# Attention steps of one head and 128 queries in a hybrid trunk layer, with gates, conv taps and weight sums moved

## The chip, the cores and the metric

The kernel runs on one core of one Trainium2 chip. The metric is the device time of one launch in microseconds (us), taken several times; the profile is one execution, read engine by engine: TensorE (PE, with its weight loads as PEld), VectorE (DVE), ScalarE (ACT), GpSimd (POOL) and SyncE (SP), which here only issues transfers. Each engine runs its own list of instructions in order, and the lists meet at semaphores.

## The reference, cut to what matters

```
u = layer_norm(x) * (1 + sc_m) + sh_m                       # x: 1024 tokens x 1024
z_pool, z_q, z_k, z_v, z_conv, z_gate = split(u @ w_in)     # 256, 3 x 512, 512, 3 x 1024 columns
y_pool = pool_mixer(z_pool) @ w_br_pool                     # causal means over 2, 4, 8, 16 tokens
y_attn = chunk_attention(z_q, z_k, z_v, rel_bias) @ w_br_attn   # 8 heads of 64, own chunk of 64 + 8 before
y_conv = conv_module(z_conv) @ w_br_conv                    # GLU, causal depthwise conv of 31 taps, LN, swish
gates = sigmoid(z_gate + b_gate)
merged = gates[0] * y_pool + gates[1] * y_attn + gates[2] * y_conv
x = layer_norm(ALPHA * x + g_m * (merged @ w_o))
u = layer_norm(x) * (1 + sc_f) + sh_f
x = layer_norm(ALPHA * x + g_f * (square(relu(u @ w_ff1 + b_ff1)) @ w_ff2 + b_ff2))
```

In the attention, softmax runs over the 576 keys of a chunk's band (fewer at the start), with a bias that depends on the clipped distance.

## The kernel before

All matmuls that carry precision take fp32 data cut in two fp32r parts, high and low, made by ACT (a copy that rounds) and DVE (what is left). A product of two such tensors is three matmuls: high x high, high x low, low x high (`product`, L1971). Weights come in blocks of 128 columns: SP loads one to `w_raw`, ACT cuts `w_hi`, DVE cuts `w_lo`, PE uses it in 8 x 2 x 3 = 48 matmuls of 512 columns. Raw, high and low each have two buffers, so block n + 2 is cut when PE has finished block n.

The order of the work on PE: blocks 0 to 5 (conv and pool inputs), blocks 6 to 8 (q, k, v of the first pair of heads), and then the attention, 4 pairs of 16 steps. A step `a` is one chunk of 64 queries of both heads of the pair. The 128 stationary rows hold both heads' features, with zeros where a query of one head meets the other (`q_block`; POOL writes the zeros). `scores` (L2126) are three products over up to 576 keys, in two parts of 288 where they are all there. DVE adds the bias and takes the maximum (L1523), ACT takes Exp and the sum (L997), DVE inverts and scales (L1537, L1538), PE transposes (L2158), ACT and DVE cut the transposed probabilities (`pt_hi`, `pt_lo`, L1544), and every second step `weigh` (L2161) multiplies them with v, 3 matmuls of 256 columns for each block of 128 keys; ACT copies two 64-row pieces out. Between these, `between` (L2209) puts matmuls that project the next pair, 9 in a step, half after the scores and half after the transposes; in the last pair they are those of two gate blocks (`EARLY = 2`), 6 in a step. Within a step, PE's order is scores(a), fillers, weigh, transposes of a - 1, fillers.

DVE also runs the 62 conv taps (L1428, 128 x 1024 each): 9 before the attention and nearly all others in its steps, but not in those after which a block is cut.

After the attention PE does a third early gate block, the pool matmuls and the conv sums, then for each of 8 output columns of 128 (j) three gate blocks and one block of branch weights. Gates 0 to 2 go through ACT's sigmoid (`gate`), DVE multiplies the branch results in PSUM with them and adds. The last column is written out by hand, with branches ahead of gates.

POOL makes the pooling means before the attention, and from the first branch results on it makes the weight sums of the second MLP matrix for a Winograd form: 16 steps (L772 to L791) each load 1 MB of `w_ff2`, scale it by the gate row (two products of 128 x 1024, L778), make four sums of 128 x 512 and store 1.75 MB to `tw_scratch`. The MLP then reads them.

Semaphores named below: `biased`, `probs_done`, `pt_lo_done` (steps of the attention), `w_lo_done` (blocks cut), `h_free` (a projection's bank read), `sig_done`, `y_used`, `tw_stored`.

## Time and profile before

| | us |
|---|---|
| median of 3 runs | 1448.37 (1446.94 to 1448.57) |
| span of the profiled execution | 1445.0 |
| time of the runs beside that span (median) | 3.4 more |
| TensorE clock granted, mean over the span | 0.999 of full |
| first scores of the attention, scores of its last step | 156.8, 386.2 |
| POOL's first and last product of the weight sums | 453.6, 659.6 |

The span goes from the first to the last instruction of the profile; a run's time holds also what lies around it. The profile names instructions by line of the kernel and by the tensors that they write and read. A PE row's duration includes the time in which the matmul drains and overlaps with the next, so the price of a matmul is the distance between the starts of two rows. For the other engines a duration is nearly the time that the instruction holds its engine, waits on a shared port included.

### The profile page before, as it was taken

What the parts mean: (1) busy time and instruction counts of PE and PEld (TensorE: products, weight loads), DVE (VectorE), ACT (ScalarE), POOL (GpSimd) and SP (SyncE); (2) the same over time, 40 slices, a digit from 0 to 9 for tenths busy, and PEclk for the clock granted to TensorE, in tenths of its full rate; (3) what the DMA queues carried; (4) which work ended last, traced back from release to release, by engine and by line L of the source; (5) the groups of instructions that cost most, each with busy time, mean ns of one, the idle gap of its engine ahead of it and who ended that gap; (6) DMA issues with size and microseconds to landing.
All of it is one profiled execution on the core that took longest, in us unless ns stands there. A gap on an engine that the chain in (4) does not pass through costs nothing.

```text
span 1445.0 us, 17546 instructions
## 1 busy us (share of the span) xinstructions
PE 1426.1 (99%) x6770; PEld 1175.9 (81%) x6770; DVE 966.1 (67%) x1242; ACT 586.8 (41%) x829; POOL 455.4 (32%) x381
## 2 busy tenths in 40 slices
PE   7999999999999999999999999999999999999997
PEld 1788888888878888888888898888888888888886
DVE  4888888887785355453468888666555744575594
ACT  3412455555562112112435765444444544443251
POOL 1003500000004889895014415533443302040011
PEclk9999999999999999999999999999999999999999
DMA  9873111101014676776451283544445868576361
GB/s 349 295 265 114 31 30 38 38 16 32 16 44 162 245 259 249 255 268 218 131 204 59 88 277 131 175 154 160 156 137 192 277 243 306 210 233 231 113 224 58
DMA packets 149267, 241.49 MB, mean 167 GB/s; under 512 B 9480, under 2 KB 79550, under 8 KB 147144
## 3 DMA queue, kind: packets, MB, share of 16 engines
q1 hardware_dynamic: 134968, 177.04, 36.7%
q0 software_dynamic: 14224, 63.45, 11.6%
q8 instruction: 47, 0.77, 0.2%
q14 instruction: 28, 0.23, 0.1%
HBM read 170.17 MB, written 70.29 MB: 166 GB/s over the span
## 4 chain that ended last, share of the span: by engine, by line
PE 96%; DVE 1%; DMA 1%; SPq 1%; ACT 0%; issue 0%; DVEq 0%
PE ps L1974 27%; PE ps L1976 27%; PE ps L1975 27%; PE ps L2102 10%; PE ps L2158 2%; DMA mid<-in_x_dram 1%; PE ps L2041 1%; PE ps L2328 0%; SPq L455 0%; DVE bn L1331 0%; PE ps L1993 0%; PE ps L2123 0%; PE ps L2017 0%; PE ps L2200 0%; PE ps L2194 0%; PE ps L2022 0%
## 5 line engine op out<-in xcount | busy, mean ns | idle before, releaser
L1974 PE MATMUL ps<-act_hi,w_hi 128*128 128x512 f32 (+1 forms) x512 | 198.0, 387 | 0.0
L1976 PE MATMUL ps<-act_hi,w_lo 128*128 128x512 f32 (+1 forms) x512 | 196.0, 383 | 0.0
L1975 PE MATMUL ps<-act_lo,w_hi 128*128 128x512 f32 (+1 forms) x512 | 195.9, 383 | 0.0
L1839 DVE TENSOR_TENSOR part_lo<-k_raw,part_hi 128x1024 fp32r<-128x1024 f32 x112 | 153.9, 1414 | 48.2 <-ACT part_hi L872 46.5
L1974 PE MATMUL ps<-part_hi 128*128 128x512 f32 x448 | 174.3, 389 | 0.0
L1975 PE MATMUL ps<-part_lo,part_hi 128*128 128x512 f32 x448 | 174.3, 389 | 0.0
L1976 PE MATMUL ps<-part_hi,part_lo 128*128 128x512 f32 x448 | 174.3, 389 | 0.0
L872 ACT ACTIVATE part_hi<-k_raw 128x1024 fp32r<-128x1024 f32 x112 | 116.3, 1059 | 108.6 <-DMA k_raw<-tw_scratch 84.5
L1571 DVE TENSOR_TENSOR w_lo<-w_raw,w_hi 128x1024 fp32r<-128x1024 f32 x30 | 73.1, 2436 | 123.9 <-ACT w_hi L872 123.8
L1974 PEld LDWEIGHTS ps<-act_hi,w_hi 128*128 128x128 f32 x512 | 96.2, 188 | 19.7 <-issue 1.4
L1975 PEld LDWEIGHTS ps<-act_lo,w_hi 128*128 128x128 f32 x512 | 96.3, 188 | 19.1 <-issue 0.7
L1976 PEld LDWEIGHTS ps<-act_hi,w_lo 128*128 128x128 f32 x512 | 96.2, 188 | 18.9
L1975 PEld LDWEIGHTS ps<-part_lo,part_hi 128*128 128x128 f32 x448 | 84.1, 188 | 17.6
L1974 PEld LDWEIGHTS ps<-part_hi 128*128 128x128 f32 x448 | 84.1, 188 | 17.4
L1976 PEld LDWEIGHTS ps<-part_hi,part_lo 128*128 128x128 f32 x448 | 84.1, 188 | 17.4
L2102 PE MATMUL ps<-act_lo,w_hi 128*128 128x512 f32 x224 | 92.0, 411 | 0.0
L1251 ACT ACTIVATE h_buf<-h_buf,cols 128x1024 f32<-128x1024 f32 x28 | 32.3, 1152 | 144.7 <-DVE h_buf L1834 144.7
L2102 PE MATMUL ps<-act_hi,w_hi 128*128 128x512 f32 x224 | 90.7, 405 | 0.1
L2102 PE MATMUL ps<-act_hi,w_lo 128*128 128x512 f32 x224 | 87.9, 392 | 0.0
L872 ACT ACTIVATE w_hi<-w_raw 128x1024 fp32r<-128x1024 f32 (+1 forms) x53 | 55.6, 1049 | 78.4 <-PE ps L1976 77.3
L1974 PE MATMUL ps<-act_hi,set_hi 128*128 128x512 f32 x224 | 87.1, 389 | 0.0
L1975 PE MATMUL ps<-act_lo,set_hi 128*128 128x512 f32 x224 | 87.1, 389 | 0.0
(261 smaller groups left out, 3243.3 us busy)
## 6 DMA issues: line engine op xcount, KB each, us to landing
k_raw<-h_scratch SPq DMA_DIRECT2D x112, 256.0 KB, 4.0
k_raw<-tw_scratch SPq DMA_DIRECT2D x112, 256.0 KB, 5.0
ada<-in_w_ada_dram SPq DMA_DIRECT2D x11, 2048.0 KB, 8.8
w_raw<-in_w_in_dram SPq DMA_DIRECT2D x42, 512.0 KB, 4.2
tw_rows<-in_w_ff_dram POOLq DMA_DIRECT2D x16, 1024.0 KB, 5.5
tw_scratch<-tw_rows POOLq DMA_DIRECT2D x16, 1024.0 KB, 4.2
h_scratch<-h_sum POOLq DMA_DIRECT2D x64, 256.0 KB, 2.8
pair_raw<-in_w_ff_dram SPq DMA_DIRECT2D x13, 1024.0 KB, 6.0
```

What stands on the lines that cost most here:

```text
L872: return nc.scalar.activation(out, in_, ACT.Copy, **kw)
L1251: nc.scalar.activation(row, row, ACT.Relu, bias=cols[:, R_FF1 + n:R_FF1 + n + 1]).then_inc(relu_done, 1)
L1571: nc.vector.tensor_tensor(w_lo[b % 2][:, :, :], w_raw[b % 2][:, :, :], f(w_hi[b % 2][:, :, :]), ALU.subtract).then_inc(w_lo_done, 1)
L1839: nc.vector.tensor_tensor(part_lo[s][:, :, :], k_raw[rs][:, :, :], f(part_hi[s][:, :, :]), ALU.subtract)\
L1974: nc.tensor.matmul(out, sh, mh, start=first, stop=False)
L1975: nc.tensor.matmul(out, sh, ml, start=False, stop=False)
L1976: return nc.tensor.matmul(out, sl, mh, start=False, stop=last)
L2041: ins = nc.tensor.transpose(ps[:, 2 * (k % 2) + i // 4, (i % 4) * P:(i % 4 + 1) * P], mid[:, i, k * P:(k + 1) * P], ident[:, :])
L2102: ins = nc.tensor.matmul(ps[:, hz % 2, :], s, v, start=kk == 0, stop=kk == 23)
L2158: ins = nc.tensor.transpose(banks(6)[:, b * P:(b + 1) * P], probs[a % 2][:, cs], ident[:, :])
```

## The change

Attention:
- A step is now one head and 128 queries (64 steps again: 4 pairs x 2 heads x 8 tiles). Widths are 128, 256, 384, 512 and then 640 keys; the corners that a chunk may not see get a bias of -1e30, written once by POOL to `bias_rev`.
- `qs` holds the high part of q in the head's 64 rows and the low part in the other 64 rows. `kd` holds k high and k low, each in all 128 rows: ACT and DVE write the head's rows, and two transfers a half (`double_keys`, SP) copy them to the other rows. The scores are two matmuls: stacked q with k high, stacked q with k low. (The product low x low is in it now.)
- `vs` holds v high and v low of a head side by side as 128 stationary columns; `pt` holds the high and low transposed probabilities side by side as 256 moving columns. `weigh` is one matmul for a block of keys and runs in every step. Its result has three useful quarters, which ACT (`take_low`) and DVE (`add_o`, two adds) bring together.
- The scaling by the inverse sum moves from DVE to ACT. All conv taps leave the attention. The fillers of the last pair are three gate blocks, 9 in a step as in the others; a fourth gate block fills the two steps in which the pipeline drains.

Behind the attention:
- The gate blocks of columns 0 to 6 (21, of which 3 are in the attention) all come ahead of the branches. Their sigmoids go to DRAM (`sig_scratch`) and come back two columns ahead (`gate_back`). Loops that counted in registers are written out.
- The taps run in the first ten gate blocks (`TAPS_IN`), the conv sums ahead of blocks 12 and 14. Then come 7 branch blocks one after another, then the last column as before.
- The weight sums start as soon as the pooling means are done and the gate row is in DRAM, inside the attention. They run in 32 half steps of 256 columns with two buffers: two products of 128 x 512 and four sums of 128 x 256 each, two loads and two stores.

The core of the diff:

```diff
+EARLY = N_BRANCH
+BR_ORDER = (0, 1, 2, 3, 6, 7, 4, 5)
+MEAN_BLOCK, VAR_BLOCK = 12, 14
+TAPS_IN = {0: 5, 1: 2, **{g: 7 for g in range(2, 9)}, 9: 6}
...
+    qs = [at(f"qs{i}", [P, 2, SEQ], f32r, X + 24 * i * KB) for i in range(2)]
+    kd = [at(f"kd{i}", [P, 2, 2, SEQ], f32r, X + (24 * i + 8) * KB) for i in range(2)]
+    vs = [at(f"vs{i}", [P, ST, 2 * P], f32r, X + (48 + 8 * i) * KB) for i in range(2)]
...
+    pt = at("pt", [P, 2, BAND_BLOCKS, 2, P], f32r, X + 74 * KB)
...
+            def double_keys(pair):
+                t = f(kd[pair % 2][:, :, :, :])
+                for half in range(2):
+                    sp.wait_ge(h_free[half], 3 * pair + 2)
+                    cs = slice(half * HALF, (half + 1) * HALF)
+                    for h in range(2):
+                        sp.dma_start(t[head_rows(1 - h), :, h, cs], t[head_rows(h), :, h, cs]).then_inc(kd_in, 16)
...
+            def store_sigmoid(m):
+                sp.wait_ge(sig_done, m + 1)
+                sp.dma_start(sig_dram[m], gate[m % N_BRANCH][:, :]).then_inc(sig_stored[m % N_BRANCH], 16)
+            def load_sigmoid(m):
+                slot = m % (2 * N_BRANCH)
+                sp.wait_ge(*sigmoids_stored(m))
+                if m < N_BRANCH:
+                    sp.wait_ge(conv_done, 2)
+                    sp.wait_ge(tw_stored, 32 * TW_STEPS)
+                elif m < 2 * N_BRANCH:
+                    sp.wait_ge(*sigmoids_stored(m + N_BRANCH * (LAST - 2)))
+                else:
+                    sp.wait_ge(y_used, m - 2 * N_BRANCH + 1)
+                sp.dma_start(gate_back[slot][:, :], sig_dram[m]).then_inc(gate_back_in[m // N_BRANCH % 2], 16)
+            for m in range(N_BRANCH):
+                store_sigmoid(m)
+            for g in range(G_BLOCKS):
+                store_sigmoid(N_BRANCH + g)
+                load_block(N_G + 4 + g)
+            for m in range(2 * N_BRANCH):
+                load_sigmoid(m)
+            for j in range(LAST):
+                if j + 2 < LAST:
+                    for b in range(N_BRANCH):
+                        load_sigmoid(N_BRANCH * (j + 2) + b)
+                load_block(N_BR + 4 + j)
...
+            def load_rows(u):
+                c, p = divmod(u, FF_PAIRS)
+                for i in range(2):
+                    r0 = (2 * p + i) * P
+                    rows = w_ff2[0, r0:r0 + P, :].rearrange("r (h n) -> r h n", h=2)[:, :, c * PIECE:(c + 1) * PIECE]
+                    nc.gpsimd.dma_start(tw_rows[u % 2][:, 2 * i:2 * i + 2, :], rows).then_inc(tw_in, 16)
...
+            pool.wait_ge(scratch_stored, 48)
+            pool.wait_ge(means_summed, 8)
+            load_piece(0)
             load_rows(0)
-            for p in range(FF_PAIRS):
-                rows, n = rows_of(p), 6 * p
+            for u in range(TW_STEPS):
+                c, p = divmod(u, FF_PAIRS)
+                rows, sums, n, cs = tw_rows[u % 2], tw_sum[u % 2], 6 * u, slice(c * PIECE, (c + 1) * PIECE)
                 b11, b12, b21, b22 = (rows[:, i, :] for i in range(4))
-                pool.wait_ge(tw_in, 16 * (p + 2))
+                pool.wait_ge(tw_in, 32 * (c + 1) + 32 * (u + 1))
                 for i in range(2):
                     pair = rows[:, 2 * i:2 * i + 2, :]
...
+                    nc.gpsimd.tensor_tensor(pair, pair, gate_piece[:, :, :], ALU.mult).then_inc(tw_summed, 1)
                 pool.wait_ge(tw_summed, n + 2)
-                nc.gpsimd.tensor_tensor(tw_sum[:, 0, :], b12, b11, ALU.subtract).then_inc(tw_summed, 1)
+                if u == FF_PAIRS - 1:
+                    load_piece(1)
+                if u >= 1:
+                    pool.wait_ge(tw_stored, 32 * u)
+                if u + 1 < TW_STEPS:
+                    load_rows(u + 1)
+                nc.gpsimd.tensor_tensor(sums[:, 0, :], b12, b11, ALU.subtract).then_inc(tw_summed, 1)
...
                 pool.wait_ge(tw_summed, n + 6)
-                nc.gpsimd.dma_start(tw_dram[p, :, 4:7, :], tw_sum[:, :, :]).then_inc(tw_stored, 16)
+                nc.gpsimd.dma_start(tw_dram[p, :, 4:7, cs], sums[:, :, :]).then_inc(tw_stored, 16)
...
+                    for h in range(2):
+                        rows = head_rows(h)
+                        ins = copy(kd[pair % 2][rows, 0, h, cs], src[rows, :])
+                    ins.then_inc(half_hi, 1)
...
+            def take_low(b):
+                pair, h, t = step_of(b)
+                act.wait_ge(pv_done, b + 1)
+                if b == STEPS:
+                    act.wait_ge(pooled_done, 4)
+                copy(mid[head_rows(h), 2 + pair, t * P:(t + 1) * P], o_bank(b, head_rows(1 - h), 0)).then_inc(o_low_done, 1)
+            def take_pt_hi(b):
+                nb = blocks_of(step_of(b)[2])
+                act.wait_ge(pt_done, b + 1)
+                if b >= 2:
+                    act.wait_ge(pv_done, b - 1)
+                copy(pt[:, b % 2, 0:nb, 0, :], banks(6)[:, 0:nb * P].rearrange("p (b q) -> p b q", q=P))\
+                    .then_inc(pt_hi_done, 1)
             for a in range(N_STEPS + 2):
-                pair, i = divmod(a, STEPS)
+                pair, h, t = step_of(a)
                 if a < N_STEPS:
-                    col, cs = a % (2 * STEPS), prob_cols(i)
+                    col, w = a % STAT_COLS, width_of(t)
                     act.wait_ge(biased, a + 1)
-                    nc.scalar.activation(probs[a % 2][:, cs], probs[a % 2][:, cs], ACT.Exp,
+                    nc.scalar.activation(probs[a % 2][:, 0:w], probs[a % 2][:, 0:w], ACT.Exp,
                                          bias=neg_max[:, col:col + 1], scale=-1.0,
                                          accum_out=row_sum[:, col:col + 1]).then_inc(exp_done, 1)
+                if a >= 2:
+                    take_low(a - 2)
                 if 1 <= a <= N_STEPS:
...
+                    take_pt_hi(a - 1)
+                if a < N_STEPS:
+                    act.wait_ge(inv_done, a + 1)
+                    copy(probs[a % 2][:, 0:w], probs[a % 2][:, 0:w], scale=inv_sum[:, col:col + 1])\
+                        .then_inc(probs_done, 1)
+                if a < N_STEPS and h == 0 and t < 2:
+                    take_v(pair, t)
+                if half_of(a):
+                    take_half(*half_of(a))
...
+            for g in range(1, G_BLOCKS):
+                act.wait_ge(g_done, g + 1)
+                take_sigmoid(N_BRANCH + g, banks(2 * (g % 2)))
+                cut_hi(N_G + 2 + g)
...
+            def add_o(b):
+                pair, h, t = step_of(b)
+                rows = head_rows(h)
+                out = mid[rows, 2 + pair, t * P:(t + 1) * P]
+                dve.wait_ge(o_low_done, b + 1)
+                nc.vector.tensor_tensor(out, o_bank(b, rows, 0), out, ALU.add).then_inc(o_added, 1)
+                dve.wait_ge(o_added, 2 * b + 1)
+                nc.vector.tensor_tensor(out, o_bank(b, rows, 1), out, ALU.add).then_inc(o_added, 1)
...
+            taps = iter(range(2 * TAPS))
+            for g in range(G_BLOCKS):
+                cut_lo(N_G + 2 + g)
+                if g == 1:
+                    for k in BR_ORDER[:4]:
+                        cut_branch_lo(k)
+                for n in itertools.islice(taps, TAPS_IN.get(g, 0)):
+                    conv_tap(n)
...
+                    for term in range(2):
+                        ins = nc.tensor.matmul(ps[:, 4 + part, 0:n], qs[s][:, h, t * P:(t + 1) * P], kd[s][:, term, h, ks],
+                                               start=term == 0, stop=term == 1)
...
+            def weigh(b):
+                pair, h, t = step_of(b)
+                s, nb = pair % 2, blocks_of(t)
+                pe.wait_ge(pt_lo_done, b + 1)
+                if b % STEPS == 0:
                     pe.wait_ge(vt_free, 2 * pair + 2)
-                if tile >= 1:
-                    pe.wait_ge(o_copied, 2 * tile)
-                else:
+                if b >= 2:
+                    pe.wait_ge(o_added, 2 * (b - 1))
+                elif b == 0:
                     pe.wait_ge(zp_done, 2)
...
+                for m in range(nb):
+                    ins = nc.tensor.matmul(ps[:, 2, (b % 2) * 2 * P:(b % 2 + 1) * 2 * P], vs[s][:, t + 1 - nb + m, h * P:(h + 1) * P],
+                                           pt[:, b % 2, m, :, :], start=m == 0, stop=m == nb - 1)
...
+                ks = range(KT) if (i, part) == (0, 0) else range(KT // 2) if (i, part) == (0, 1) else range(KT // 2, KT)
+                if (i, part) == (1, 1):
+                    return
+                h = int((i, part) != (0, 0))
+                if ks[0] == 0:
+                    pe.wait_ge(w_lo_done, N_G + 1)
+                    pe.wait_ge(h_free[h], 3 * (PAIRS + 1))
+                ins = gate_half(N_G, 0, h, ks)
+                if i == 1:
+                    ins.then_inc(g_done, 1)
...
+            for g in range(1, G_BLOCKS):
+                bank = 2 * (g % 2)
+                if g == 1:
                     mix_pool()
...
+                elif g == MEAN_BLOCK:
+                    pe.wait_ge(pm_scaled, 4)
+                    pe.wait_ge(tap_done, 2 * TAPS + 1)
+                    conv_sums(4, conv_sum)
+                elif g == VAR_BLOCK:
+                    pe.wait_ge(squared, 3)
+                    conv_sums(6, sq[:, 0, :])
+                pe.wait_ge(w_lo_done, N_G + g + 1)
+                if g == 1:
+                    pe.wait_ge(o_added, 2 * N_STEPS)
+                    pe.wait_ge(vt_free, 2 * PAIRS)
+                else:
+                    pe.wait_ge(sig_done, g + 2)
+                gate_half(N_G + g, bank, 0)
+                gate_half(N_G + g, bank, 1).then_inc(g_done, 1)
...
+                n = N_BR + j
+                pe.wait_ge(w_lo_done, n + 1)
+                for y, (k0, k1, bank) in enumerate(((0, 2, 4), (2, 6, 6), (6, 8, 2))):
+                    if j >= 1:
+                        pe.wait_ge(y_used, 3 * (j - 1) + y + 1)
```

## Rows read from the trace of the kernel before

**Rows 1.** The page, part 1: busy time of each engine.

```profile
PE 1426.1 (99%) x6770; PEld 1175.9 (81%) x6770; DVE 966.1 (67%) x1242; ACT 586.8 (41%) x829; POOL 455.4 (32%) x381
```

**Rows 2.** Windows of 50 us: length, busy us (xstarts) by engine, granted clock, DMA.

```profile
450.00:500.00 50.00, 50.00 (x222) 41.39 (x221) 19.00 (x9) 8.53 (x9) 42.05 (x29) 1.00 0.66 238
```

**Rows 3.** Timeline in the attention: start, us, engine, line, operation, count, [idle].

```profile
156.77 0.19 PE L1974 MATMUL ps<-k_hi,q_hi 128*128 128x64 f32 x1
...
372.79 0.19 PEld L1974 LDWEIGHTS ps<-pt_hi,v_hi 128*128 128x128 f32 x1 [0.66 <-DVE pt_lo L1544]
...
386.19 0.29 PE L1974 MATMUL ps<-k_hi,q_hi 128*128 128x288 f32 x1
...
386.98 0.40 PE L2102 MATMUL ps<-act_hi,w_hi 128*128 128x512 f32 x1
...
388.04 0.28 PE L1975 MATMUL ps<-pt_lo,v_hi 128*128 128x256 f32 x1
...
389.70 0.71 PE L2158 MATMUL ps<-ident,probs 128*128 128x128 f32 x5
...
390.17 0.48 PE L2102 MATMUL ps<-act_hi,w_hi 128*128 128x512 f32 x1
```

**Rows 4.** Groups of ACT by form, 157 to 390 us: xcount, busy, mean, idle.

```profile
L997 ACT ACTIVATE probs<-probs,neg_max 128x576 f32<-128x576 f32 x32 | 24.9, 778 | 50.9 <-DVE neg_max L1523 50.9
...
L872 ACT ACTIVATE pt_hi<-ps 128x640 fp32r<-128x640 f32 x30 | 21.0, 702 | 13.4 <-PE ps L2158 13.3
...
L872 ACT ACTIVATE mid<-ps 64x128 f32<-64x128 f32 x60 | 16.0, 266 | 0.7
...
L872 ACT ACTIVATE w_hi<-w_raw 128x1024 fp32r<-128x1024 f32 x11 | 11.6, 1056 | 0.1
...
L872 ACT ACTIVATE q_hi<-ps 64x512 fp32r<-64x512 f32 x12 | 7.1, 591 | 0.5 <-PE ps L2102 0.4
```

**Rows 5.** Groups of DVE by form, 157 to 392 us.

```profile
L1428 DVE SCALAR_TENSOR_TENSOR mid<-h_pad,cols,mid 128x1024 f32<-128x1024 f32 x47 | 60.1, 1279 | 0.0
...
L1544 DVE TENSOR_TENSOR pt_lo<-ps,pt_hi 128x640 fp32r<-128x640 f32 x31 | 25.5, 822 | 13.1 <-ACT pt_hi L872 13.0
...
L1523 DVE CUSTOM_DVE_ANT_0 probs<-ps,bias_rev 128x576 f32<-128x576 f32 x32 | 24.1, 752 | 1.3 <-PE ps L1976 1.3
...
L1538 DVE TENSOR_SCALAR probs<-probs,inv_sum 128x576 f32<-128x576 f32 x32 | 16.7, 521 | 1.1
...
L1325 DVE TENSOR_TENSOR w_lo<-w_raw,w_hi 128x1024 fp32r<-128x1024 f32 x11 | 13.4, 1216 | 0.0
```

**Rows 6.** POOL's weight sums: one line's min/median/max ns, then groups.

```profile
L778 POOL TENSOR_TENSOR tw_rows<-tw_rows,gate_row x32: 2389/2404/3404, 453.6 to 659.6; 128x1024 f32<-128x1024 f32 x32
...
L783 POOL TENSOR_TENSOR tw_sum<-tw_rows 128x512 f32<-128x512 f32 x16 | 21.2, 1326 | 1.8 <-DMA tw_scratch<-tw_sum 1.4
...
L767 POOL DMA_DIRECT2D tw_rows<-in_w_ff_dram x16 | 12.3, 771 | 13.7 <-DMA tw_scratch<-tw_sum 13.7
...
L789 POOL DMA_DIRECT2D tw_scratch<-tw_rows x16 | 9.2, 576 | 0.0
```

**Rows 7.** Timeline of POOL: the last pooling means.

```profile
159.10 0.51 POOL L727 TENSOR_TENSOR mid<-mid 64x16 f32<-64x16 f32 x2
```

**Rows 8.** Timeline of DVE and POOL side by side in the gate blocks.

```profile
555.84 1.23 DVE L1602 TENSOR_TENSOR tmp<-ps,gate 128x1024 f32<-128x1024 f32 x1
...
557.17 1.30 DVE L1609 TENSOR_TENSOR mid<-mid,tmp 128x1024 f32 x1
...
557.45 2.16 POOL L785 TENSOR_TENSOR tw_sum<-tw_rows,tw_sum 128x512 f32<-128x512 f32 x1
...
558.39 2.31 DVE L1571 TENSOR_TENSOR w_lo<-w_raw,w_hi 128x1024 fp32r<-128x1024 f32 x1
```

**Rows 9.** DMA issues: count, KB each, median us from issue to landing.

```profile
ada<-in_w_ada_dram SPq DMA_DIRECT2D x11, 2048.0 KB, 8.8
...
tw_scratch<-tw_rows POOLq DMA_DIRECT2D x16, 1024.0 KB, 4.2
```

More of the change, by code:

```diff
@@ new lines, in _ @@
+            act.wait_ge(g_done, 1)
+            take_sigmoid(N_BRANCH, banks(0))
+            cut_hi(N_G + 2)
+            for u in range(4):
+                t, half = divmod(u, 2)
+                act.wait_ge(pm_done, u + 1)
+                copy(mid[:, t, half * HALF:(half + 1) * HALF], ps[:, MIX_BANKS[u], :],
+                     scale=cols[:, R_PSC + t:R_PSC + t + 1]).then_inc(pm_scaled, 1)
+            act.wait_ge(pm_scaled, 4)
+            act.wait_ge(sig_done, N_BRANCH)
+            act.wait_ge(o_added, 2 * N_STEPS)
@@ L1111, in cut_row_hi @@
+            for j in range(LAST):
+                cut_hi(N_BR + 2 + j)
             def cut_row_hi(k):
```

921 lines of the change are left out of this document (351 added, 570 removed).

## Prediction

> **What bounds the kernel now.** The page comes first: TensorE (PE) is busy 99% of the span [rows 1]. Its matmuls overlap, so busy time says little; I read the windows of 50 us for how many matmuls start in each [rows 2]. Where all are 512 columns wide, as in the one shown, 222 start in 50 us, 0.225 us apart: PE has no holes there, and each column taken off it is time. Then the PE timeline inside the attention [rows 3], for what narrow matmuls really cost from start to start; the waits in the same stretch, for how near PE is to waiting; last, ScalarE (ACT), VectorE (DVE) and GpSimd (POOL) by form [rows 4 to 6], since the change gives PE less to do while they must keep up. PE is the bound everywhere, with little spare in the last pair of heads: there weigh waits 0.66 us for pt_lo [rows 3].
>
> **PE work removed.** Prices from [rows 3], start to start: six score products of 288 columns take 386.98 - 386.19 = 0.79, so 0.132 each; fourteen of 256 take 389.70 - 388.04 = 1.66, so 0.119. Between 256 and 512 columns I interpolate (0.00041 a column: 320 cost 0.145, 384 0.172, 448 0.199); below 256 I take 0.11.
> - Scores before, a pair: three products at each of the widths 64 to 512, 3 x 1.19 = 3.57, and 8 x 6 x 0.132 = 6.34; times 4 pairs 39.6. After, a head: two products at 128, 256, 384, 512, 2 x 0.626 = 1.25, and 4 steps x 4 x 0.145 = 2.32; times 8 heads 28.6. **-11.0.**
> - Weighing before: 120 blocks x 3 x 0.119 = 42.8. After: 240 x 1 x 0.119 = 28.6. **-14.3.**
> - The 240 transposes, all projections, gates, branches and fp32 sums remain; 48 gate matmuls move into the last pair, another 48 fill the two drain steps. 0.
> Together **-25.3**, certain to about 1.
>
> **Attention, the other engines.** A full step now asks 4.27 us of PE (9 fillers 2.05, scores 0.79, half a weighing 0.89, transposes 0.54), and 3.59 in the last pair, which has 6 fillers. After, it is 2.05 + 4 x 0.145 + 5 x 0.119 + 0.54 = 3.77 in all pairs. Against that stands a ring through DVE and ACT, in their program order: bias 0.82 (the 576-wide one takes 0.75; 640 is as wide as pt_lo), 0.12 for the accumulator and handing over, Exp 0.86 (0.778 x 640/576) and 0.10, o_low 0.25, pt_hi 0.70, 0.05, pt_lo 0.76, then the next bias: 3.66 [rows 4, 5]. The scaling of probs on ACT (some 0.73) and add_o lie beside it. So the ring has 0.1 us a step to spare. Taps are gone from it (before: bias, tap, reciprocal, scale, pt_lo, 3.5 of DVE against 3.59 in the last pair, and it waited there; over a = 0 to 62, 229.4 us from the first scores at 156.77 to those at 386.19, my prices give 225.6, so about 3.8 of waits [rows 3]).
> What a step carries besides now has no room: the w_lo cut (1.22) is in the ring, the w_hi cut (1.06) and the 64-row copies (0.59 each, and k takes two where it took one) hold up the next Exp by about 1.25. A pair has 3 x (1.2 + 1.25) + 2 x 0.8 = 9, and POOL, which now works here, makes each w_lo cut wait some 0.5: 10.5. The narrow steps of each head give back about 2.5 (their rings are 1.9 to 2.9, PE 2.7 to 3.4), and 0.8 lies ahead of weigh. Some 4 a pair remain: 16 of waits where 3.8 were, **+12**. Bounds: 0 (waits stay as they are) and +30 (nothing is given back).
> double_keys, two q/k transfers and bias loads a head lie on SP, five steps ahead of use; a 256 KB transfer between block loads is not late. 0.
>
> **Gate blocks, where taps meet weight sums.** All 62 taps now run in DVE's block iterations 0 to 9 behind the attention, seven in most: 7 x 1.28 + 1.22 = 10.2 of a block's 48 x 0.225 = 10.8. Alone they fit. But POOL's weight sums run from about 161 us (the means end at 159.6 [rows 7], the first weights arrive) and both engines wait for one another where both read two tensors in SBUF: an add of 1.3 us, then a sum of 1.3 that takes 2.16 and a cut of 1.22 that takes 2.31, in strict turns, while the product ahead of them, which reads PSUM, stays at 1.23 [rows 8]. The Trainium skill ("SBUF — State Buffer", "SBUF: two separate sides") says that the two share one pair of ports as an exclusive lock for a whole instruction; by this rule, which speaks against taps beside sums, the trace agrees.
> How long POOL needs: a 1024-wide product is 2.39 alone, a 512-wide sum 1.30, so 256 wide is 0.75 [rows 6]. A half step has 2 x 1.30 + 4 x 0.75 = 5.6, gaps 0.3, two loads 1.54, two stores 1.1 and a wait for the stores of about 0.8: 9.4; if an issue costs more for rows cut in pieces (0.77 against 0.57 for twice the pieces [rows 6]) 10.5; with no wait 8.5. 32 of them at 9.4 plus 0.3 for cuts: done at 471. The attention with its drain ends at 156.8 + 624 x 0.228 + 28.6 + 28.6 + 26.4 + 3.5 + 16 = 402, taps start 8 later behind four sigmoids and a cut, at 410, when (410 - 161)/9.7 = 25.7 half steps are done and **6.3** are left.
> Each takes from DVE 2.4 (two products back to back) + 4 x 0.6 = 4.8. DVE's own work from iteration 0 to the cut of iteration 9 is 10 cuts, 56 taps, 4 branch cuts: 90 from block 0's end + 7, done at +97; PE wants that cut at 3.0 (pooling) + 10 x 10.8 = +111. So PE waits 4.8 x 6.3 - 14 = **+16**. Bounds: 0 (2.9 half steps left, or taps win the ports), and +30, since in 140 us of turns POOL gets through no more than nine.
> One sentence of its own: the skill ("DMA: Bandwidth & Descriptors", "Anatomy of one DMA — SWDGE (gpsimd) path") gives a transfer issued by GpSimd 2.0 us and its bytes at 436 GB/s; by that an estimate of the stores' wait is 1.2 instead of 0.8, a half step 9.8, one more is left, and the sum is some 5 higher; the trace has 4.2 from issue to landing for 1 MB [rows 9].
>
> **Branches.** The sigmoids come back from DRAM. SP stores the last one 1.2 after the last gate block, then waits for the w_lo cut (+3.5), loads one block and three tiles: 2 MB. 2 MB in one piece land in 8.8 [rows 9]; I take 8 after the first issue, at +12, the product takes 1.22, and PE wants its bank at +10.8: **+2.5**, 0 to 6. Afterwards a block gives DVE 6 operations of 1.22 in 10.8, and refills of 2 MB run one block ahead: 0. The last column's gates, w_o and the MLP are as before.
>
> **Sum.** 1445.0 - 25.3 + 12 + 16 + 2.5 = 1450.2 for the span; the median of the runs lies 3.4 above the span of the profile: **1454**. A difference within 0.2% (2.9 us, 1445.5 to 1451.3) is about what a measurement of this kernel can't tell from no change.
>
> **Rivals.**
> 1. All is hidden but the start of the branches: the ring's lateness is absorbed as it is now in pairs 0 to 2, and taps lose nothing. 1448.4 - 25.3 + 2.5 = **1426**. For it: DVE loses the taps in attention, some 60 us [rows 5]. Against: the ring's 3.66 to 3.77. Chance 0.17.
> 2. Only the gate blocks go well (POOL ends by about 440, or taps hold the ports since they follow one another at once): 1448.4 - 25.3 + 12 + 2.5 = **1438**. Decides at 2.9 half steps left, that is 8.6 us a half step. Against: the turns in [rows 8]. Chance 0.20.
> 3. Gains and waits cancel, within 0.2%: five half steps left instead of 6.3. Chance 0.15.
> 4. The ring sets the attention: nothing is given back in narrow steps, +30, POOL at its cap +25: **1480**. For it: ACT has 2.7 a full step and 2.3 more where halves and cuts meet. Chance 0.10.
> My forecast, slower at 1451.3 to 1468, has 0.38. Slower in all 0.48, the same 0.15, faster 0.37. Range 1426 to 1472, leaving the far end of 4 and part of 1; that of the forecast alone is 1451 to 1468. The sides are near to each other because 25 certain us stand against two waits that each can be nothing.
>
> **What the profile after would show.** Right: PE matmuls of the attention some 25 us less; weigh and scores waiting for pt_lo and biased just behind each w_lo cut; POOL's sums reaching beyond 460 us; taps of 1.9 us in the mean instead of 1.28 in the first seven iterations, with blocks of 14 to 16 us on PE waiting for w_lo; one wait of 2 to 3 us on the first refill. Wrong: POOL done near 430, or taps at 1.28 beside it; windows of 222 matmuls from the first gate block on; attention waits under 5 us. It would also be wrong if a half step of sums cost 8 us or less, if lateness in the ring vanished in the narrow steps, or if PE's prices for 320 columns were not on the line between 256 and 512.

## The result, and the profile after

The changed kernel takes **1483.2 us** (median of 4, 1478.7 to 1485.7) against 1447.9 for the kernel before: ratio **1.024, 95% interval 1.022 to 1.026**, slower. The forecast was 1454, the range ended at 1472. The side was right, the size was not: it lost 35 us where 6 were forecast.

The page, part 1, of the kernel after (the answer to [rows 1]):

```profile
PE 1419.0 (96%) x6554; PEld 1157.4 (78%) x6554; DVE 998.1 (67%) x1314; ACT 635.3 (43%) x902; POOL 550.0 (37%) x553
```

PE has fallen from 99% to 96% busy: it now has holes. The windows show where (length, busy us and starts by engine, granted clock, DMA). [Rows 2] had 222 starts in 50 us:

```profile
450.00:500.00 50.00, 42.97 (x176) 34.34 (x175) 49.36 (x27) 8.25 (x8) 41.91 (x37) 0.93 0.47 161
500.00:550.00 50.00, 40.97 (x164) 32.57 (x163) 49.29 (x28) 6.18 (x6) 37.25 (x33) 0.93 0.53 188
```

DVE is busy for 49 of the 50 us in both windows and POOL for 42 and 37, PE starts 176 and 164 matmuls, and its granted clock has fallen too. The waits from 150 to 640 us (who waited for whom, total, times, longest):

```profile
POOL tw_rows L786 <- DMA tw_scratch<-tw_sum: 60.2, 29, 3.7
...
POOL gate_piece L777 <- DMA gate_scratch<-gate_ff: 23.3, 1, 23.3
PEld ps L2135 <- DVE pt L1515: 22.6, 24, 1.9
PEld ps L1942 <- DVE w_lo L1313: 21.3, 7, 4.4
PE ps L1942 <- DVE w_lo L1313: 18.3, 7, 4.0
POOL tw_scratch L813 <- issue: 16.4, 12, 2.7
```

PE waits for pt_lo (line 1515) in the attention and for w_lo (line 1313) in the gate blocks, and POOL waits 60 us for its own stores. The groups of DVE (xcount, busy, mean of one, idle):

```profile
L1416 DVE SCALAR_TENSOR_TENSOR conv_acc<-h_pad,cols,conv_acc 128x1024 f32<-128x1024 f32 x60 | 109.8, 1831 | 1.8
L1313 DVE TENSOR_TENSOR w_lo<-w_raw,w_hi 128x1024 fp32r<-128x1024 f32 x52 | 77.3, 1486 | 62.4 <-ACT w_hi L888 62.4
```

A tap takes 1.83 in the mean where [rows 5] had 1.28.

**Where the 36 us are.** To add up PE's losses I took each PE start and subtracted the price of the matmul before it, with the prediction's prices. What is left over is waiting, matmuls at the lower clock, and a floor that is there without any wait (9.5 in the attention in the best run below). Between the marks of the timeline (first scores, last weigh, first branch product, first product of w_o):

| | before | after | difference |
|---|---|---|---|
| first scores at | 156.8 | 164.7 | +7.9 |
| over the prices, in the attention | 10.9 | 28.3 | +17.4 |
| over the prices, from its end to the branches | 0.6 | 27.5 | +26.9 |
| over the prices, in the branches | 0 | 5.3 | +5.3 |
| first scores to first product of w_o | 570.1 | 597.7 | +27.6 |
| from there to the end of the span | 718.1 | 718.5 | +0.4 |

27.6 less the three stages' 49.6 leaves -22.0 for PE's work. Nothing is lost behind the branches. The attention's figure is good to a few us only. Matmuls that start sooner than their price, as some do behind a wait, pull the sum down, and how they are counted matters: with all of them counted at the prediction's prices the three stages are 21.6, 26.4 and 4.9 longer, and the -25.3 for the work comes out by construction.

### The profile page after: what moved, and what is told of

Its sections match the earlier page's. It is cut to its first block, busy times and chain, and to the rows that moved or that the text cites. A ratio compares the mean times of both kernels' runs of the same rounds, so it can differ in the third digit from the quotient of the medians.

```text
span 1480.9 us, 17398 instructions
## 1 busy us (share of the span) xinstructions
PE 1419.0 (96%) x6554; PEld 1157.4 (78%) x6554; DVE 998.1 (67%) x1314; ACT 635.3 (43%) x902; POOL 550.0 (37%) x553
## 4 chain that ended last, share of the span: by engine, by line
PE 71%; DVE 17%; ACT 6%; issue 3%; DMA 2%; SPq 1%; POOL 0%; DVEq 0%; ACTq 0%; POOLq 0%
PE ps L1942 22%; PE ps L1944 21%; PE ps L1943 21%; DVE conv_acc L1416 7%; PE ps L2070 3%; DVE w_lo L1313 3%; DVE probs L1497 1%; DVE partial L1358 1%; ACT probs L1024 1%; DMA mid<-in_x_dram 1%; ACT pt L888 1%; ACT mid L888 1%; DVE pt L1515 1%; PE ps L2135 1%; ACT probs L888 1%
## 5 line engine op out<-in xcount | busy, mean ns | idle before, releaser
L1942 PE MATMUL ps<-act_hi,w_hi 128*128 128x512 f32 (+1 forms) x496 | 196.1, 395 | 18.3 <-DVE w_lo L1313 18.3
L1943 PE MATMUL ps<-act_lo,w_hi 128*128 128x512 f32 (+1 forms) x496 | 192.5, 388 | 0.0
L1944 PE MATMUL ps<-act_hi,w_lo 128*128 128x512 f32 (+1 forms) x496 | 192.2, 388 | 0.0
L1313 DVE TENSOR_TENSOR w_lo<-w_raw,w_hi 128x1024 fp32r<-128x1024 f32 x52 | 77.3, 1486 | 62.4 <-ACT w_hi L888 62.4
L1416 DVE SCALAR_TENSOR_TENSOR conv_acc<-h_pad,cols,conv_acc 128x1024 f32<-128x1024 f32 x60 | 109.8, 1831 | 1.8
L2070 PE MATMUL ps<-act_lo,w_hi 128*128 128x512 f32 x240 | 100.3, 418 | 0.0
L2070 PE MATMUL ps<-act_hi,w_hi 128*128 128x512 f32 x240 | 96.0, 400 | 4.0 <-DVE kd L1461 2.9
L888 ACT ACTIVATE w_hi<-w_raw 128x1024 fp32r<-128x1024 f32 x53 | 55.8, 1054 | 93.7 <-PE ps L1944 92.7
L2070 PE MATMUL ps<-act_hi,w_lo 128*128 128x512 f32 x240 | 94.5, 394 | 0.0
L1048 ACT ACTIVATE gate<-ps,cols 128x1024 f32<-128x1024 f32 x21 | 23.4, 1114 | 149.2 <-PE ps L1944 148.5
```

The costliest lines, as they stand in the source:

```text
L888: return nc.scalar.activation(out, in_, ACT.Copy, **kw)
L1048: nc.scalar.activation(gate[b][:, :], src, ACT.Sigmoid, bias=cols[:, R_GATE + 8 * b + j:R_GATE + 8 * b + j + 1]).then_inc(sig_done, 1)
L1313: nc.vector.tensor_tensor(w_lo[n % 2][:, :, :], w_raw[n % 2][:, :, :], f(w_hi[n % 2][:, :, :]), ALU.subtract).then_inc(w_lo_done, 1)
L1416: nc.vector.scalar_tensor_tensor(out=acc, in0=src, scalar=w, in1=acc, op0=ALU.mult, op1=ALU.add)\
L1942: nc.tensor.matmul(out, sh, mh, start=first, stop=False)
L1943: nc.tensor.matmul(out, sh, ml, start=False, stop=False)
```

## The experiments

The theory: GpSimd's weight sums are behind most of it. They take turns with VectorE's operations on two SBUF tensors, and since a half step is longer than priced, more of them meet the taps. The rivals: VectorE has simply too much to do, transfers are late, or the new ring of the attention is at fault by itself. The kernel before had medians of 1447.2 to 1448.5 beside these runs. Each edit is against the changed kernel.

**e1, taps spread thinner.**

```diff
-MEAN_BLOCK, VAR_BLOCK = 12, 14
-TAPS_IN = {0: 5, 1: 2, **{g: 7 for g in range(2, 9)}, 9: 6}
+MEAN_BLOCK, VAR_BLOCK = 13, 15
+TAPS_IN = {0: 5, 1: 2, **{g: 5 for g in range(2, 7)}, **{g: 6 for g in range(7, 12)}}
```

> The taps of the changed kernel are spread thinner: 5 a gate block in blocks 2 to 6 and 6 in blocks 7 to 11 where it has 7 in blocks 2 to 8 and 6 in block 9; the sums of the layer norm of the convolution come one block later. The work is the same. Theory (taps and weight sums take turns): a tap beside the sums takes 1.9 us, so 5 of them and a cut of 1.3 to 2.9 take 10.9 to 12.5 us of a block of 10.8, with 14 us of lead at the start; of the 27 us that TensorE now waits for w_lo in the gate blocks 0 to 6 stay: 1456 to 1464 us. Rival (VectorE is not what is short there, the transfers or the cut of w_hi are): the waits move with the blocks and the time stays within 4 us of 1483.

Measured 1476.2 (1472.9 to 1483.5), ratio 1.019 [1.017, 1.021]: a miss. The gate blocks behaved nearly as expected (10.4 over the prices, from 27.5), but in the profiled execution, the slowest of its four, the attention, which the edit doesn't touch, had 42.1 where 28.3 were. The timelines of DVE, POOL and PE show one such place:

```profile
211.67 4.03 DVE L1313 TENSOR_TENSOR w_lo<-w_raw,w_hi 128x1024 fp32r<-128x1024 f32 x1
```

```profile
212.08 2.53 POOL L799 TENSOR_TENSOR tw_rows<-tw_rows,gate_piece 128x512 f32<-128x512 f32 x2
```

```profile
216.50 1.44 PE L2110 MATMUL ps<-kd,qs 128*128 128x320 f32 x4 [2.46 <-DVE neg_max L1497]
```

The w_lo cut, 1.22 alone, takes 4.03: it ends 1.1 us after GpSimd's two products that run back to back, so it let both pass. The biases stand behind it in VectorE's queue, and PE waits 2.46. Whether a cut meets the products is a matter of phase, and the executions of the kernels with full sums in the attention spread by 4 to 16 us, those of the kernel before by 3.

**e2, no sums.** The products and the four sums (lines 799 to 812) work on 8 columns, each as the one shown; the second store sends rows in place of sums, the same bytes.

```diff
-nc.gpsimd.tensor_tensor(sums[:, 0, :], b12, b11, ALU.subtract).then_inc(tw_summed, 1)
+nc.gpsimd.tensor_tensor(sums[:, 0, 0:8], b12[:, 0:8], b11[:, 0:8], ALU.subtract).then_inc(tw_summed, 1)
...
-nc.gpsimd.dma_start(tw_dram[p, :, 4:7, cs], sums[:, :, :]).then_inc(tw_stored, 16)
+nc.gpsimd.dma_start(tw_dram[p, :, 4:7, cs], rows[:, 0:3, :]).then_inc(tw_stored, 16)
```

> GpSimd's products and sums of the second weights are left out but for 8 columns of each (the transfers, their sizes and their waits stay; the weights stored are the raw ones, so the second half's numbers are not those of the reference). Theory (waiting for one another's operands): the 27 us of waits for w_lo in the gate blocks vanish wholly; of the attention's some 17 us of waits those vanish that come from lengthened cuts (w_lo 1.49 in the mean for 1.22), a third: about 1450 us, 1444 to 1456. If the ring of the attention needs no help of GpSimd to be late: 1456 with all 17 us left. Rival (GpSimd's transfers, not its sums, are what disturbs): 1475 or more.

Measured 1449.2, ratio 1.001 [1.000, 1.002]: as expected, 34 us less. The gate blocks have 1.2 over the prices; the attention still has 22.3. This trace shows one thing more. The timeline of POOL:

```profile
241.93 1.50 POOL L786 DMA_DIRECT2D tw_rows<-in_w_ff_dram  x2 [3.48 <-DMA tw_scratch<-tw_rows]
...
246.24 0.77 POOL L813 DMA_DIRECT2D tw_scratch<-tw_rows  x1 [1.85 <-issue]
...
251.98 1.49 POOL L786 DMA_DIRECT2D tw_rows<-in_w_ff_dram  x2 [3.79 <-DMA tw_scratch<-tw_rows]
```

With almost nothing to compute a half step still takes 11.1 us in the attention, where it takes 11.3 with the sums: its length isn't that of the sums.

**e3, no taps.**

```diff
-src, acc = h_pad[:, t, tap:tap + SEQ], conv_acc[:, t, :]
+src, acc = h_pad[:, t, tap:tap + (8 if tap else SEQ)], conv_acc[:, t, 0:8 if tap else SEQ]
```

> All taps but the first of each half work on 8 of 1024 columns (the convolution is left out in effect); GpSimd's sums stay. Theory: the waits for w_lo of the gate blocks (27 us with what the lower clock behind them costs) vanish, the attention stays as it is: 1456 us, 1453 to 1460; GpSimd's half steps keep 11.4 us behind the attention where they take 14.2 now, and its last sum ends at about 530 us in place of 550. Rival (the sums or transfers alone hold VectorE's cut back): 1470 or more.

Measured 1458.4, ratio 1.008 [1.006, 1.009], as expected: gate blocks 1.3, attention 26.1. So the 27 us need both taps and sums. VectorE alone, and transfers alone, cost nothing there.

**e4, the second window sums later.**

```diff
 pool.wait_ge(pooled_done, 2)
+pool.wait_ge(partial_done, 12 - N_DIRECT)
```

> The one edit: GpSimd's second group of window sums waits for the same partial of the adaptive rows as in the kernel before, so that it runs beside the end of the first projections (from about 144 us) and not beside VectorE's rows 11 (124 to 139 us). Theory (before the attention, too, it is the turns: 7 rows took 7.0 and 7.5 us for 5.5, and a cut 2.9 for 1.2): TensorE's waits of 1.2 us for q and 3.1 us for the keys and the lower clock behind them vanish, minus 0 to 2 for weight sums that start later: 1475 to 1478 us. Rival (the second cut of the keys, 1.4 us for 0.7, and the wider copies on ScalarE make it late): 1481 to 1484 us.

Measured 1478.3 (1473.8 to 1480.0), ratio 1.021 [1.018, 1.023]. The first scores start at 158.0 in place of 164.7, and VectorE's rows, shown next as they are in the changed kernel, are back at 5.48 us: the cause of this part is shown. The time is just above the 1475 to 1478 of the theory. The cause is one that the prediction didn't have. The changed kernel no longer clears q, so GpSimd goes on to its second group of window sums at 123.6, where they ran at 143.4 before. The timeline of DVE in the changed kernel:

```profile
120.62 6.99 DVE L1358 SCALAR_TENSOR_TENSOR partial<-ada,c_act,partial 128x512 f32<-128x512 f32 x7
127.52 2.91 DVE L1313 TENSOR_TENSOR w_lo<-w_raw,w_hi 128x1024 fp32r<-128x1024 f32 x1
...
132.77 7.46 DVE L1358 SCALAR_TENSOR_TENSOR partial<-ada,c_act,partial 128x512 f32<-128x512 f32 x7
```

Seven rows take 7.0 and 7.5 us (5.48 in the kernel before), the cut 2.9. The next cut of the keys is late, and PE waits (timeline of PE):

```profile
150.39 0.47 PE L2070 MATMUL ps<-act_hi,w_hi 128*128 128x512 f32 x1 [2.94 <-DVE kd L1461]
...
151.41 0.63 PE L2070 MATMUL ps<-act_hi,w_hi 128*128 128x512 f32 x1
151.84 0.63 PE L2070 MATMUL ps<-act_lo,w_hi 128*128 128x512 f32 x1
```

Behind the wait matmuls start 0.43 apart for 3.4 us, and not 0.23: the granted clock is 0.50 from 150.9 to 154.0, the lower of its two levels (1.2 GHz). The wait of 2.9 costs 4.7 in all.

**e5, the wait for the stores moved behind three sums.**

```diff
-if u >= 1:
-    pool.wait_ge(tw_stored, 32 * u)
-if u + 1 < TW_STEPS:
-    load_rows(u + 1)
 nc.gpsimd.tensor_tensor(sums[:, 0, :], b12, b11, ALU.subtract).then_inc(tw_summed, 1)
...
 nc.gpsimd.tensor_tensor(b12, b22, b12, ALU.subtract).then_inc(tw_summed, 1)
+if u >= 1:
+    pool.wait_ge(tw_stored, 32 * u)
+if u + 1 < TW_STEPS:
+    load_rows(u + 1)
```

> The one edit: in each half step of the weight sums GpSimd waits for the stores of the step before, and loads the next weights, behind three of the four sums and not ahead of them. Theory (the length of a half step, 11.4 us, decides how many are left for the taps): the wait of some 2 us for stores shrinks to under 0.5, a half step takes 9.5 to 10, 4 fewer than 9 are left when the taps start, at 3 us or so each: 1467 to 1474 us. Rival (the next weights are now late instead, or the sums win nothing because VectorE pays for each of them wherever they fall): 1480 to 1486 us.

Measured 1496.0 (1486.0 to 1499.6), ratio 1.032 [1.027, 1.036]: slower than either view had it, and a half step went from 11.3 to 11.8. The timeline of POOL in this run:

```profile
268.54 1.49 POOL L786 DMA_DIRECT2D tw_rows<-in_w_ff_dram  x2 [0.89 <-DMA tw_scratch<-tw_sum]
270.05 0.74 POOL L812 TENSOR_TENSOR tw_sum<-tw_rows,tw_sum 128x256 f32<-128x256 f32 x1
273.10 0.79 POOL L813 DMA_DIRECT2D tw_scratch<-tw_rows  x1 [2.31 <-issue]
```

The wait didn't go, it moved: the sums are done at 270.8, but the store isn't issued until 273.1, 0.34 us after the second load has landed. In this trace that wait came 31 times, 90 us in all, and each time the store was issued 0.34 to 0.37 us behind the landing. So GpSimd's queue took the stores only when the loads were through, and by the code the loads wait for the stores. A half step is a chain of transfers, not of sums. An estimate from the changed kernel's rows: the loads are issued 0.73 behind the last store's landing, the second one 0.75 later, it lands in 3.4, the first store follows 0.34 behind it, the second 0.78 later, and it lands in 4.7, 10.7 in all for the 11.3 measured.

**e6, cuts in other slots of the attention.**

```diff
-if r in (1, 3, 5):
+if r in (1, 3, 5) and pair == 0:
     cut_hi(N_P1 + 3 * pair + part + 2)
...
+if half_of(a - 1) and half_of(a - 1)[1] % 2:
+    late_pair, late_r = half_of(a - 1)
+    cut_hi(N_P1 + 3 * late_pair + late_r // 2 + 2)
 if half_of(a):
     take_half(*half_of(a))
...
     add_scores(a)
+if half_of(a - 2) and half_of(a - 2)[1] % 2:
+    cut_lo_after(*half_of(a - 2))
...
-elif half_of(a - 1) and half_of(a - 1)[1] % 2:
-    cut_lo_after(*half_of(a - 1))
```

> The one edit: inside the attention ScalarE cuts w_hi one step later, and VectorE cuts w_lo behind the biases of the next step, where it waits for the exponential anyhow, in place of behind pt_lo. Theory (the attention's some 17 us of waits come where the 1.2 of a cut and the 1.1 of a w_hi cut stand in the ring): 12 places give back up to 1 us each on VectorE, and as much on ScalarE: the waits of the attention fall to 8 or less, 1471 to 1477 us. Rival (the waits come from GpSimd holding up whatever reads SBUF there, so they only move): 1480 to 1486 us.

Measured 1478.1 (1472.1 to 1485.2), ratio 1.020 [1.016, 1.025], 1 us beyond the far end of what the theory gave. The attention fell from 28.3 to 22.9 over the prices, but the gate blocks rose to 31.3: the first tap comes earlier and finds 10 half steps left and not 9.

**e7, the first sigmoids loaded back one block earlier.**

```diff
 for g in range(G_BLOCKS):
+    if g == G_BLOCKS - 2:
+        for m in range(N_BRANCH):
+            load_sigmoid(m)
     store_sigmoid(N_BRANCH + g)
```

> The one edit: the first three sigmoids are loaded back while gate block 16 runs, not behind the last block's load. Theory (the branches' first product waits for the last of these loads): the wait of 3.6 us and the 1.7 us of lower clock behind it vanish: 1477 to 1479 us against 1483. Rival (the first product's 1.2 us and the bank are what TensorE waits for): 1482 to 1484 us.

Measured 1477.8 (1475.4 to 1479.9), ratio 1.021 [1.019, 1.023], as expected; the branches' 5.3 are 0.0.

**e8, e1 and e4 to e7 together.**

> Taps spread, second means late, stores' wait behind the sums, cut slots and early sigmoids together. Theory: each pays its own part, before the attention 7, attention 8 to 10, gate blocks 25, branches 5, minus 0 to 4 for overlaps: 1436 to 1444 us, below the kernel before. Rival (the waits go from one place to the next, as those of the spread taps did, 7 us for an expected 20): 1455 to 1465 us.

Measured 1460.6, ratio 1.010 [1.007, 1.012]: the rival's number. The attention has 15.6 and the branches 0, but the half steps, with e5's order in them, last until 560 us, and PE waits 15.8 for the sum of the taps.

**e9, loads on another queue.** SyncE issues loads 1 to 31 between its block loads; GpSimd waits for its stores before it issues the next ones.

```diff
+def load_ff2(u):
+    sp.wait_ge(tw_summed, 6 * (u - 1) + 2)
+    if u >= 2:
+        sp.wait_ge(tw_stored, 32 * (u - 1))
...
+        sp.dma_start(tw_rows[u % 2][:, 2 * i:2 * i + 2, :], rows).then_inc(rows_in, 16)
+ff2_before = {12: (1,), 13: (2, 3, 4), 14: (5, 6), 15: (7, 8), 16: (9, 10, 11), 17: (12,), 18: (13, 14, 15),
+              19: (16, 17, 18), 20: (19, 20), 21: (21, 22, 23), 22: (24, 25), 23: (26, 27, 28), 24: (29, 30)}
...
+for u in ff2_before.get(n, ()):
+    load_ff2(u)
 load_block(n)
```

> The one edit: 31 of the 32 loads of second weights are issued by SyncE, between its own block loads, in place of GpSimd; products, sums and stores stay where they are. Theory (a half step of 11.4 us is set by GpSimd's own queue: its loads wait until its stores have landed, 2.0, and, as moving the load showed, its stores aren't issued until its loads have landed, 2.3 to 3): with loads on another queue a half step is 2.55 + 3.2 + 1.55 and at most a us more, 7.5 to 8.5; GpSimd ends at 410 to 440 us, before or just after the first tap, and the 27 us of waits in the gate blocks go to under 4; the attention may pay 2 to 4 us for denser turns: 1456 to 1463 us. Rival (a half step stays near 11 because each sum waits its turn, or the transfers themselves are slow): 1474 or more.

Measured 1476.5, ratio 1.021 [1.017, 1.025]: a miss by 13, at the rival's number, though not for the rival's reason. A half step fell to 9.0 us, and not one wait was left among the taps, but PE waited once for 18.2 us: a block's w_lo at the first gate blocks, held up on SyncE by loads that weren't due.

**e10, the same with the parts of e4, e6 and e7.**

> Second weights loaded by SyncE, the second window sums beside the end of the first projections, the cuts' slots in the attention and the early sigmoids, together; the taps stay as in the changed kernel. Theory: minus 25 (gate blocks), 6 (ahead of the attention), 6 (ring), 5 (branches) from 1483, plus 0 to 4 for denser turns: 1440 to 1446 us, that is 2 to 8 us below the kernel before. Rival (a wait removed in one stage comes back in the next): 1450 to 1460 us.

Measured 1465.6, ratio 1.011 [1.010, 1.013]: a miss by 20, with one wait of 26.7 for w_lo and one of 8.9 for the copies of the keys, both behind loads on SyncE.

**e11, no sums, and the slots of e6.**

> GpSimd's products and sums left out but for 8 columns (as before, the stored weights are raw), and the two cuts of the attention in their later slots. The run without sums alone gave 1449 us, with some 13 us of waits in the attention. Theory (what is left there is the ring: the cuts and 64-row copies stand in it): the slots take at least two thirds of it: 1438 to 1442 us. Rival (what is left is the wait for the first steps of each head and the halves of q and k, which the slots don't touch): 1446 to 1449 us.

Measured 1435.3 (1434.2 to 1435.8), ratio 0.991 [0.990, 0.993]: beyond what the theory gave. The attention has 9.5 over the prices, and only two waits over 0.25 us. The four executions lie within 1.5 us of each other. With the sums left out but the cuts in their old slots (e2) ten lay within 4.9.

**e12 and e13, loads placed anew,** by the times at which e10's half steps wanted them (the diff is against e9); e12 has the other parts too, e13 doesn't.

```diff
+ff2_before = {12: (1,), 13: (2, 3), 14: (5,), 15: (6, 7), 16: (8, 9), 17: (11,), 18: (12, 13, 14),
+              19: (15, 16), 20: (18, 19), 21: (20, 21), 22: (22, 23), 23: (24, 25), 24: (26, 27)}
+ff2_before_keys = {14: 4, 17: 10, 20: 17}
...
+load_ff2(28)
 for m in range(N_BRANCH):
     store_sigmoid(m)
+load_ff2(29)
...
     load_block(N_G + 4 + g)
+    if g < 2:
+        load_ff2(30 + g)
```

> As the run with SyncE loads, slots, late means and early sigmoids, with the 31 loads placed anew in SyncE's order, so that neither the copies of the keys nor the stores of the sigmoids stand behind a load that isn't due. Theory (the waits of 26.7 and 8.9 us there were for this order alone): 1465.6 minus 26.7 and 8.9 is 1430, plus 0 to 6 for half steps that now run beside the first taps: 1430 to 1437 us, 0.8 to 1.2% under the kernel before. Rival (the sums so pushed meet more of VectorE's cuts and taps, and the time comes back there): 1442 to 1450.

> The changed kernel with only the loads of second weights on SyncE, placed as in the other run of this pair. Theory: the half step of 8.8 us in place of 11.4 takes the waits in the gate blocks from 27 us to 0 to 5 and leaves the others (8 ahead of the attention, 17 in it, 5 at the branches): 1456 to 1461 us. Rival (denser turns in the attention cost what the gate blocks gain): 1468 or more.

e13: 1460.1 (1455.6 to 1462.9), ratio 1.009 [1.007, 1.011], as expected: only the queue of the loads is changed, and with it the place where GpSimd waits for its stores, and the gate blocks go from 27.5 to 6.2. e12: 1447.0 (1439.5 to 1451.3), ratio 0.999 [0.998, 1.000]: a miss, with a wait of 12.7 for w_lo.

**e14, GpSimd takes back the last four loads** (against e12).

```diff
-load_ff2(28)
-load_ff2(29)
...
+OWN_FROM = 28
...
+if OWN_FROM <= u + 1 < TW_STEPS:
+    pool.wait_ge(tw_stored, 32 * u)
+    load_rows(u + 1)
```

> As the version with all edits, but the last four loads of second weights are issued by GpSimd itself again, so that nothing stands ahead of the sigmoids' stores on SyncE. Theory: the wait of 12.9 us at the second gate block vanishes; four half steps of 11 us run to about 445 us, three of them beside taps, 14 us against 14 of lead: 0 to 5 us of waits: 1433 to 1439 us, 0.6 to 1.0% under the kernel before. Rival (the sums' turns take it back): 1443 to 1448.

Measured 1446.4 (1441.0 to 1456.8), ratio 0.999 [0.997, 1.000]: a miss again. I had looked for the wait in the wrong loads. The timelines of ACT and SP in this run show who it is:

```profile
415.39 1.11 ACT L1077 ACTIVATE gate<-ps,cols 128x1024 f32<-128x1024 f32 x1 [14.27 <-DMA sig_scratch<-gate]
416.41 1.05 ACT L914 ACTIVATE w_hi<-w_raw 128x1024 fp32r<-128x1024 f32 x1
```

```profile
399.55 8.32 SPq L552 DMA_DIRECT2D tw_rows<-in_w_ff_dram  x4
407.92 0.60 SPq L474 DMA_DIRECT2D w_raw<-in_w_in_dram  x1
408.57 2.23 SPq L577 DMA_DIRECT2D sig_scratch<-gate  x3
```

ScalarE has the three sigmoids at 401.1, SyncE stores them at 408.6 behind two loads and a block. The fourth sigmoid waits for a buffer that is free only when the first of these stores has landed, at 415.4, and the cut of w_hi stands behind it.

**e15, these stores ahead of the last loads and the last block, and the taps spread as in e1** (against e14).

```diff
+if n == N_G + 3:
+    for m in range(N_BRANCH):
+        store_sigmoid(m)
 for u in ff2_before.get(n, ()):
     load_ff2(u)
 load_block(n)
```

> As the run before it, with the stores of the first three sigmoids ahead of the last two loads and the last block load on SyncE, and the taps spread to 5 and 6 a block over blocks 0 to 11. Theory: the wait of 8.3 us vanishes, the three of 9 us fall to 0 to 4 (thinner taps beside the last five half steps): 1433 to 1440 us, 0.6 to 1.0% under the kernel before. Rival (the waits move again): 1443 to 1448.

Measured **1433.2** (median of 6, 1429.7 to 1437.8), ratio **0.990 [0.989, 0.992]**: faster than both kernels, at the near end of what was expected. Its page and windows:

```profile
PE 1403.2 (98%) x6554; PEld 1153.0 (81%) x6554; DVE 968.2 (68%) x1314; ACT 635.9 (44%) x902; POOL 504.7 (35%) x499
```

```profile
450.00:500.00 50.00, 48.60 (x213) 39.58 (x212) 49.34 (x30) 8.93 (x9) 33.84 (x28) 1.00 0.57 181
500.00:550.00 50.00, 48.32 (x210) 39.01 (x209) 37.47 (x30) 11.76 (x12) 0.00 (x0) 1.00 0.28 95
```

PE starts 213 and 210 matmuls where it started 176 and 164, and its clock is whole. Over the prices it has 10.6 in the attention, 7.1 in the gate blocks, 0 in the branches; the first scores start at 159.2.

## Why the prediction was wrong, step by step

| step | predicted | the trace |
|---|---|---|
| PE work | -25.3 | -22.0 as what is left over (-24 in e11 and e15, which have few waits) |
| ahead of the attention | 0 | +7.9 |
| waits of the attention | +12 | +17.4 (up to +21.6, by how it is added up) |
| gate blocks | +16 | +26.9 |
| branch start | +2.5 | +5.3 |
| the rest | 0 | +0.4 |
| sum on the span | +5.2 | +35.9 |

**PE work: right.** Four products of 320 columns take 0.59, 0.147 each, where 0.145 was interpolated, and those of 256 still 0.12. In e15 first scores to first product of w_o take 552.0 for 570.1 in the kernel before, with 6.2 more over the prices: -24.3, within the 1 us that was allowed.

**Gate blocks: the mechanism right, the length of a half step wrong.** This is the step that failed and did most of the harm. I added up GpSimd's own operations and a wait of 0.8 to "9.4", with ends of 8.5 and 10.5; it takes 11.3, and the path that sets it is another one: the transfers, one behind the other, with the sums hidden beside them (e2, e5). The timeline of POOL in the changed kernel:

```profile
224.50 2.55 POOL L799 TENSOR_TENSOR tw_rows<-tw_rows,gate_piece 128x512 f32<-128x512 f32 x2
228.57 1.50 POOL L786 DMA_DIRECT2D tw_rows<-in_w_ff_dram  x2 [1.52 <-DMA tw_scratch<-tw_sum]
230.09 1.49 POOL L807 TENSOR_TENSOR tw_sum<-tw_rows 128x256 f32<-128x256 f32 x1
231.65 0.74 POOL L809 TENSOR_TENSOR tw_sum<-tw_rows,tw_sum 128x256 f32<-128x256 f32 x1
232.35 0.74 POOL L810 TENSOR_TENSOR tw_rows<-tw_rows 128x256 f32<-128x256 f32 x1
233.17 0.73 POOL L812 TENSOR_TENSOR tw_sum<-tw_rows,tw_sum 128x256 f32<-128x256 f32 x1
234.36 0.79 POOL L813 DMA_DIRECT2D tw_scratch<-tw_rows  x1 [0.45 <-issue]
235.14 0.76 POOL L815 DMA_DIRECT2D tw_scratch<-tw_sum  x1
```

Products 2.6 and sums 0.75 each were priced right. The stores' issue is 1.55 for 1.1. The wait for stores, 0.8 in my sum, is 1.5 here and 60.2/29 = 2.1 in the mean, and the wait ahead of the store I didn't have at all. I took the wait over from [rows 6], where a full step's longer sums and products cover more of the transfers' time; cutting steps in half doubles the number of such round trips and halves their cover. By the formula in the Trainium skill ("DMA: Bandwidth & Descriptors", "Anatomy of one DMA — SWDGE (gpsimd) path") the prediction's estimate of this wait was 1.2; the trace has 2.1. GpSimd also starts at 167.8 and not 161, since the gate row comes from the late partials (161.6 in e4). So the first tap, at 428.5, finds 23 half steps started and **9 left, not 6.3**; by the prediction's own formula 4.8 x 9 - 14 = 29, and 26.9 came. e13 turns this one cause off: 9.1 us a half step, three left, 6.2 over the prices. Of the 26.9, 18.3 are waits for w_lo; the lower clock behind the three longest of them is some 6.

**Turns: right, but not strict.** e2 and e3 show that only the pair of taps and sums costs. The trace agrees with the lock that the prediction cited from the Trainium skill ("SBUF — State Buffer", "SBUF: two separate sides"): an operation waits for whole instructions of the other engine. But the one that waits doesn't always get the next turn. The cut of 4.03 us let two products pass, and so, in the changed kernel itself, did one operation in every half step from 430 to 548: eight taps and one cut of branch weights took 4.0 to 4.1. The prediction's 2.4 for two products back to back had this in its price, though its text speaks of "strict turns". "POOL makes each w_lo cut wait some 0.5" was right in the mean: the 12 cuts of the attention take 1.68 for 1.22. But each stands in the ring, and a single one can cost PE 2.5 us.

**Attention: the ring was priced well.** The prediction had 16 us of waits (its own terms, 10.5 less twice 2.5 and 0.8, leave 4.7 a pair, or 19, where it went on with "some 4"). Against e11's floor of 9.5 the changed kernel has 18.8; without the sums (e2) 12.8, and without sums and with the cuts out of the ring's tight place (e11) none. So some 13 are the cuts and copies in the ring, some 6 the sums beside it, up to 20 in another execution (e1). That lateness "is given back in narrow steps" wasn't tested by itself.

**double_keys at 0 was right, the cover ahead of it wasn't.** Neither the copies nor the second cut cost more than a us: with the window sums late the scores start at 158.0 (e4), 37.3 us behind the first projection of q, which was 36.6 in the kernel before and 42.4 in the changed one. What failed is a step that the prediction doesn't have, the clearing of q, whose removal let GpSimd's window sums slide under VectorE's rows. Of the 7.9, 2.1 come earlier: that projection starts at 122.4 for 120.2. In the other runs, whose code is the same up to there, it starts anywhere from 120.3 to 123.3, so these 2.1 are no cost that can be put down to the change.

**Branch start: right place, double the size.** A wait of 3.4 was near the 2.5, but PE runs at the lower clock behind it: 5.3 in all, and e7 takes both back.

**Lower clock: not priced at all.** No term of the sum had it. In the changed kernel 3.4 to 5.1 us of PE at half rate stand behind each of the five waits of 2.9 us and more, and add 1.6 to 2.6 each time, some 9 in all; behind its waits of 1.4 to 2.3 there is no such stretch.

Of the rivals, the fourth ("the ring sets the attention, POOL at its cap") had the right size, 1480, at a chance of 0.10, but not the right parts.

## What to carry to other kernels

A cover has an end, and its length is the number to measure: when a background chain is cut into smaller pieces, price the round trips of its transfers anew, by the chain (store landed, load landed, next store), not by the sum of its operations. When work is taken off an engine early in the program, ask what now starts earlier there and whom it meets. PE work saved was worth its price in the end (e15), but only after single waits of 3 to 27 us, each behind something unrelated in a queue kept in program order, had been found one by one in the trace; a load moved to another queue must not stand ahead of anything that is due sooner.
